# Second layer of a two-layer mixture-of-experts backbone: when the first expert's down matrix and the second expert's up and gate matrices are requested

## The reference, cut to what matters

```
def run_block(args):
    xb, e = args
    return (jax.nn.silu(xb @ w1[e]) * (xb @ w3[e])) @ w2[e]
```

## Time and profile before

| | before |
|---|---|
| median of 3 runs | 2494.8 us (2493.83 to 2494.88) |
| span of the profiled execution, first to last instruction | 2493.2 us |
| PE busy | 2179.9 us (87%) |
| DVE busy | 786.5 us (32%) |
| ACT busy | 646.0 us (26%) |
| POOL busy | 183.2 us (7%) |
| read from HBM | 534.79 MB |
| SP's queue q1 | 515.42 MB, 51.9% of 16 engines' span |

### The profile page before, as it was taken

How to read it: one execution, slowest core, us unless ns; L and a number is a source line. 1 busy time by engine, 2 the same in 40 slices (tenths; PEclk the granted TensorE clock), 3 DMA queues, 4 the chain that set the end, 5 groups by cost and what they waited for, 6 DMA issues and landing times. The chain is left out here.

```text
span 2493.2 us, 35756 instructions
## 1 busy us (share of the span) xinstructions
PE 2179.9 (87%) x15496; PEld 1111.2 (45%) x15496; DVE 786.5 (32%) x1223; ACT 646.0 (26%) x1016; POOL 183.2 (7%) x126
## 2 busy tenths in 40 slices
PE   4799998969995899999999738999886999998884
PEld 3588885536673333333333224444673333332222
DVE  2423226655326111111111183565644111111104
ACT  4421105553214111111111134554422111111111
POOL 0000000000000000000000021334000000000003
PEclk7699999989997999999999858999898999999996
DMA  8201108026934989889999350000107999999996
GB/s 305 75 26 34 43 1 345 1 89 221 300 134 155 388 358 411 347 350 412 412 420 416 133 172 17 26 26 9 52 19 278 424 419 410 415 428 415 427 427 220
DMA packets 145840, 595.90 MB, mean 239 GB/s; under 512 B 25524, under 2 KB 61072, under 8 KB 120976
## 3 DMA queue, kind: packets, MB, share of 16 engines
q1 hardware_dynamic: 115568, 515.42, 51.9%
q0 software_dynamic: 11952, 43.52, 4.8%
q10 hardware_dynamic: 18160, 34.61, 3.8%
HBM read 534.79 MB, written 58.72 MB: 238 GB/s over the span
## 5 line engine op out<-in xcount | busy, mean ns | idle before, releaser
L1804 PE MATMUL ph<-w,x_t 128*32 128x512 f32 x6016 | 680.4, 605 | 39.3 <-DMA w<-in_exp_w 37.1
L1804 PEld LDWEIGHTS ph<-w,x_t 128*32 128x32 f32 x6016 | 191.8, 111 | 450.6 <-issue 426.6
L1817 PE MATMUL py<-w,g_t 128*32 128x512 f32 x3008 | 341.1, 594 | 1.0 <-DVE g_t L1923 1.0
L1917 DVE TENSOR_TENSOR hidden<-hidden,ph 64x512 f32<-64x512 f32 x94 | 102.1, 1086 | 754.8 <-ACT hidden L1875 754.8
L1875 ACT ACTIVATE hidden<-ph 64x512 f32<-64x512 f32 x94 | 55.6, 591 | 694.5 <-PE ph L1804 694.5
L2131 PE MATMUL z<-hT,w_cd 128*128 128x512 f32 (+1 forms) x448 | 183.6, 568 | 5.5 <-ACT hT L490 5.4
L1817 PEld LDWEIGHTS py<-w,g_t 128*32 128x32 f32 x3008 | 93.6, 110 | 204.9 <-issue 203.6
L708 PE MATMUL z<-h_high,w_hi 128*128 128x512 f32 (+1 forms) x432 | 161.7, 374 | 15.4 <-DVE h_low L538 15.4
L1782 POOL DMA_INDIRECT x_rows<-h_tokens,index x47 | 44.4, 945 | 1765.4 <-PE px L1789 979.8
L710 PE MATMUL z<-h_high,w_lo 128*128 128x512 f32 (+1 forms) x432 | 157.4, 364 | 0.0
L709 PE MATMUL z<-h_low,w_hi 128*128 128x512 f32 (+1 forms) x432 | 157.1, 364 | 0.0
(11 more groups left out here) (318 smaller groups left out, 2346.5 us busy)
## 6 DMA issues: line engine op xcount, KB each, us to landing
w<-in_exp_w SPq DMA_DIRECT2D x192, 2048.0 KB, 15.5
ada_raw<-in_ada_w SPq DMA_DIRECT2D x24, 2048.0 KB, 8.6
y_slots<-y_rows ACTq DMA_DIRECT2D x188, 128.0 KB, 9.1
y_slots<-zero SPq DMA_DIRECT2D x29, 512.0 KB, 14.7
h_tokens<-h_rows ACTq DMA_DIRECT2D x18, 512.0 KB, 2.6
w_ab<-in_w_in_ab SPq DMA_DIRECT2D x14, 512.0 KB, 3.7
w_cd<-in_w_in_cd SPq DMA_DIRECT2D x12, 512.0 KB, 3.7
x_t_saved<-xT SPq DMA_DIRECT2D x8, 640.0 KB, 8.1
```

Of the source, the lines that this page charges most:

```text
L1804: ins = pe.matmul(ph[row:row + UNIT, :], xt[:, k, at:at + UNIT], w13[place[2 * b + n] % RING][:, half, k, :], start=(k == 0), stop=(k == K ...
L1817: ins = pe.matmul(py[b % 2][row:row + UNIT, :], gt[:, k, n * UNIT:(n + 1) * UNIT], w2[place[2 * b + n] % RING][:, k, half * 512:(half + 1) ...
L1917: dve.tensor_tensor(hid[PAIR:P, :].rearrange("s (k q) -> s q k", k=FT), hid[0:PAIR, :].rearrange("s (q k) -> s q k", k=FT), ph[PAIR:P, :]. ...
```

## The change: what it does

In the second layer only (`layer` is 1), the requests for the first expert's down matrix and for the second expert's up and gate matrices move from the start of `experts`, where they stood behind the wait for the first gather, into `route`, right behind the request for the first expert's up and gate. The wait of SP for the first gather is gone in this layer, so SP's other early requests (second expert's down, third expert's up, gate and down) come as soon as `experts` begins. The first layer stays as it is.

```
--- before.py
+++ after.py
@@ -1508,6 +1508,9 @@
                 sp.wait_ge(s_table, 1)
                 first = self.expert_of(sp, 0)
                 self.load_up(sp, layer, ring, 0, first)
+                if layer:
+                    self.load_down(sp, layer, ring, 0, first)
+                    self.load_up(sp, layer, ring, 1, self.expert_of(sp, 1))
                 for i in range(HROWS):
                     sp.wait_ge(s_hw[i], 16 * len(range(i, nt, HROWS)))
 
@@ -1747,13 +1750,15 @@
 
             @block.sync
             def _(sp):
-                sp.wait_ge(s_x, 16)
-                self.load_down(sp, layer, ring, 0, self.expert_of(sp, 0))
+                if layer == 0:
+                    sp.wait_ge(s_x, 16)
+                    self.load_down(sp, layer, ring, 0, self.expert_of(sp, 0))
                 for j in range(1, NE):
                     e = self.expert_of(sp, j)
                     if j >= RING:
                         sp.wait_ge(s_a, last[j - RING] // 2 + 1)
-                    self.load_up(sp, layer, ring, j, e)
+                    if j > 1 or layer == 0:
+                        self.load_up(sp, layer, ring, j, e)
                     if j >= RING:
                         sp.wait_ge(s_b, last[j - RING] // 2 + 1)
                     self.load_down(sp, layer, ring, j, e)
```

## The result

The changed kernel takes 2502.66 us (median of 6 runs, 2500.43 to 2505.05) against 2494.84 us (median of 6) before: ratio 1.0027, 95% interval 1.0017 to 1.0038, that is 4.2 to 9.5 us. It is slower by 7.8 us by the medians, with 2501.3 forecast: inside the stated range (2495.0 to 2505.0), and 0.2 us above the forecast's own (2499.5 to 2502.5). A later set of runs gave 2501.0 us (9 runs) against 2494.95 us (30 runs), +6.1 us, ratio 1.0027 (1.0017 to 1.0036). The span of the profiled execution is 2499.7 us.

A forecast was written before the change was run, and what follows sets the result against it. PE was taken to bound the middle of the second layer's experts, the matrices the last 240 us. Terms +7.8 - 0.9 - 0.4 = +6.5 us gave 2501.3 us, 0.26% slower, range 2495.0 to 2505.0.

The forecast's parts named there:

- The gather's hold-up: Second layer's first gather, now beside queued weights, takes 12.0 us instead of 4.2, making PE start 7.8 us later.
- exactly the second's case: The second gather, issued at 1912.4 beside only the weight queue, took 12.5 us; the first was expected to meet the same.
- the twelve: Twelve gathers in the middle of the second layer's experts, taking 6.7 to 12.6 us, median 11.4.
- The estimate beside it: Alternative from the DMA queue-turn rule: the first gather stands behind one weight request, 5.4 us, giving +4.1 in the sum.
- short hold-up: Rival: first gather takes 6.7 us, sum +1.2 (2496.0 us); with 8 to 9 us, +2.5 to +3.8; chance 0.10.
- Pair 3's wait: PE's 0.9 us wait for the third expert's gate matrix at pair 3 disappears: -0.9 us.
- The head start is spent waiting: Weights' 9.0 us lead is lost as the fourth expert's request waits for PE's buffer; queue runs dry at 1943.7.
- PE's lateness passes to the end whole: PE stays 6.9 us late through the middle; with 0.4 returned, the weight-bound end behind 2200 is 6.5 us late.
- The emptier queue: Down requests in the PE-bound middle land about 9.4 us after issue instead of 9.8: -0.4 us.
- the six: Six down requests in the PE-bound middle, landing after 8.8 to 10.7 us, mean 9.8, taken as finding the queue all but empty.

The follow-up runs named there:

- x3: Kernel before with only SP's wait for the first gather removed in the second layer, requests staying in `experts`: 2500.21 us, +5.3 on before.
- x1: Kernel before with the second layer's first gather replaced by a POOL fill of zeros: 2490.64 us, -4.3 on before.
- x2: Changed kernel with the second layer's first gather replaced by a POOL fill of zeros: 2490.47 us, -4.5 on before.
- x11: Kernel before with the second layer's third expert's up and gate requested ahead of the second expert's down: 2495.3 us, 0.0 on before.
- x5: Kernel before with 18 matmuls on constants ahead of the second layer's first transposes, making PE alone late: 2507.94 us, +12.9 on before.
- x9: Kernel before with third expert's up and gate requested ahead of second's down, and 10 and 4 matmuls filling PE's idle time (second layer): 2489.82 us, -5.5.
- x10: Changed kernel with 10 and 12 matmuls on constants filling PE's idle time in the second layer: 2497.4 us, +2.1 on before.
- x7: Changed kernel with 20 and 24 matmuls on constants filling PE's idle time in the second layer: 2513.78 us, +18.7 on before.
- x8: Kernel before with third expert's up and gate requested ahead of second's down, and 20 and 10 matmuls in PE's idle time (second layer): 2501.27 us, +6.2.

## Why the prediction was right

- **The gather's hold-up** was the loss, as forecast. The term was 7.8 us and measured 6.9 or 7.0 (11.1 and 11.2 us against 4.2), so PE waited 12.9 us and not near 14. The prediction took the gather for "exactly the second's case" (12.5); it came out nearer to the median of the twelve, 11.4. x3 made the same loss with nothing but the contention, and x1 and x2 removed the loss with the gather. The estimate beside it, one request's turn (+4.1 in the sum), was too low: the 11.1 to 12.1 us seen are those of gathers in the middle of the stage, and the packets show one row for one piece of weights. The forecast's 7.8 us held two delays in one number, the later start (2.4 us) and the shared engines; the prediction did not tell them apart. In its short hold-up, 9 us would give +3.5 and not +3.8.
- **Pair 3's wait** went, -0.9, in the quick profile of the changed kernel; x11 shows it alone. Where PE's clock comes back late, that wait is not there to be lost.
- **The head start is spent waiting.** The last early request landed at 1939.5, 52.5 us behind the first (forecast: 51.9), and the next request came at 1948.23, 61.2 us behind it; before it came 51.4 us behind it (1943.24). x1 and x2 put its worth at 0.1 us of PE time, below any measurement.
- **PE's lateness passes to the end whole.** +6.0 at pair 4 and +6.0 at the last down in the pair of quick profiles; x5 repeats it with 14.4 and 14.3. The +9.2 of the slow pair lies 2.2 above its pair 4, within the scatter of that stretch.
- **The emptier queue** was the term that was wrong, small as it was: I took 0.4 us back because down requests would land after 9.4 us instead of 9.8. The shortest and longest of the six from 1997.1 to 2168.8 took 9.4 and 11.0 us, 10.1 in the mean, no less than before. The queue had been all but empty in the middle already, so there was nothing to gain; the last of them:

```profile
L1458 SPq DMA_DIRECT2D w<-in_exp_w x1: 333/333/333, 2168.8 to 2168.8; - x1
...
DMA to landing us min/median/max: 11.0/11.0/11.0
```

The measured terms give 6.9 - 0.9 = +6.0 us, against +7.8 and +6.1 timed; with the slow ups in both kernels pair 3 gives nothing back and it is +7.0. That the profiled span is 2499.7, just the forecast, is partly chance: its stretch ahead of the change was 4.7 us short, its slow ups cost 2.8 more than before, and its weight-bound end some 2.5 more.

## What to carry to other kernels

In this kernel a DMA share of 1.0 did not say that transfers bounded a stage. Look at the requests that wait for a freed buffer: if they land as fast as one into an empty queue, the consumer bounds it, and asking for more data ahead of time buys nothing. A small gather at the head of a stage that the whole stage hangs on should run alone; an explicit wait that keeps big loads out of its way can be worth more than the idle DMA time that it shows (here some 5 us, x3). Compare two profiles from a point just ahead of the edit, and profile the unchanged kernel twice before believing a difference of a few us.

## What the runs showed of the hardware

- A gather of 128 rows of 4 KB takes 4.2 to 4.5 us alone, 7.4 with one 2 MB request in line, 11.0 to 12.1 beside a full queue, even when the first of those requests is issued 0.1 us behind the gather (x3). Its first row moves 1.8 us after its issue alone and 4.0 to 4.8 us beside weights; beside a full queue each engine then moves one 16 KB piece of weights (0.61 us) for each 4 KB row (0.16 us).
- PE's clock comes back after its idle time at a moment that varies between executions, and in some it falls once more after the 1.8 us of waiting between the first two ups. With the same code the two took 8.5 and 7.1 us or 9.4 to 9.6 and 8.7 to 8.8 us, and in x3 and x11 9.1 to 9.3 and 7.1. With the short fillings (x9, x10) it stayed at full speed through the transposes but not through the first up (8.54 and 8.52 us); with fillings that ran up to the transposes (x5, x7, x8) the first two ups took 7.07 us each.
- A 128x512 float32 matmul on all 128 rows took 0.87 us at full clock, as two instructions; I had counted the 0.43 of one.
- Runs of the kernel before lay within 2.3 us in the first six, but over 12.3 us (2488.2 to 2500.53) in thirty later ones (12.1 us in 35 more, 13.7 in 19). Effects under about 3 us could be told only in profiles, from the first request on.
